# Two products of 256 columns in place of one of 512, three for the left half of the bank and then three for the right

## The reference, cut to what matters

```python
mix = jnp.einsum('btd,de->bte', merged, w_out[l])                   # first block: out projection
u = jnp.square(jax.nn.relu(jnp.einsum('btd,df->btf', n2, w_up[l])))
h = h + _rmsnorm(jnp.einsum('btf,fd->btd', u, w_down[l]), ...)      # F = 4096
...
mix = jnp.einsum('bse,ed->bsd', ..., w_o[layer])                    # second block, two layers
ffn = swiglu(x, w_gu_dense, w_down_dense)                           # layer 0, F = 2816
out = out + gates[..., e:e + 1] * swiglu(x, w_gu[e], w_down[e])     # layer 1, e = 0..7, two gates non-zero per token
```

## Time and profile before

| | |
|---|---|
| median of 3 runs | 1766.68 us |
| the profiled execution, its own time | 1765.85 us |
| its span in the profile | 1764.0 us |
| PE busy | 1740.7 us, 99% |
| PE weight loads busy | 1566.5 us, 89% |
| DVE busy | 1360.9 us, 77% |
| ACT busy | 1074.3 us, 61% |
| products of L449 to L451 with 512 columns | 3 x 1226 |
| of these in the experts (992 us to the end) | 3 x 992 |

### The profile page before, as it was taken

How to read it: one execution, slowest core, us unless ns; L and a number is a source line. 1 busy time by engine, 2 the same in 40 slices (tenths; PEclk the granted TensorE clock), 3 DMA queues, 4 the chain that set the end, 5 groups by cost and what they waited for, 6 DMA issues and landing times.

```text
span 1764.0 us, 26421 instructions
## 1 busy us (share of the span) xinstructions
PE 1740.7 (99%) x11201; PEld 1566.5 (89%) x11201; DVE 1360.9 (77%) x1586; ACT 1074.3 (61%) x1200; POOL 187.6 (11%) x191
## 2 busy tenths in 40 slices
PE   8999999999999999999999999999999999999997
PEld 8999999999988999998997888788888888888885
DVE  6895488677664667655687899888889898989897
ACT  7654455565544444443346778777777776777774
POOL 1454170000000100000030202100000000000110
PEclk9999999999999999999999999999999999999998
DMA  9332464656556545565463599999999999999993
GB/s 290 120 109 73 118 179 133 224 174 199 181 190 202 187 153 188 189 227 181 144 200 132 209 388 345 384 408 408 372 385 356 398 367 398 355 384 359 392 409 140
DMA packets 179542, 452.11 MB, mean 256 GB/s; under 512 B 11813, under 2 KB 119816, under 8 KB 145496
## 3 DMA queue, kind: packets, MB, share of 16 engines
q1 hardware_dynamic: 176424, 440.37, 69.3%
q0 software_dynamic: 2992, 9.98, 1.4%
HBM read 442.14 MB, written 5.79 MB: 254 GB/s over the span
## 4 chain that ended last, share of the span: by engine, by line
PE 89%; DVE 6%; ACT 3%; DMA 1%; issue 1%; SPq 0%; DVEq 0%; ACTq 0%
PE bank L449 27%; PE bank L451 27%; PE bank L450 27%; DVE ring_r L439 2%; PE bank L3283 1%; ACT hi_ring L424 1%; DMA ring<-in_expert_blocks 1%; PE bank L2545 1%; PE bank L1371 1%; PE bank L1363 1%; DVE arena L946 1%; PE bank L1855 1%; PE bank L2526 0%; PE bank L1840 0%; PE bank L2175 0%
## 5 line engine op out<-in xcount | busy, mean ns | idle before, releaser
L439 DVE TENSOR_TENSOR ring_r<-ring,hi_ring 128x2048 fp32r<-128x2048 f32 x401 | 905.7, 2283 | 257.2 <-ACT hi_ring L424 256.9
L424 ACT CAST hi_ring<-ring 128x2048 fp32r<-128x2048 f32 (+1 forms) x404 | 758.2, 1905 | 120.6 <-PE bank L451 108.8
L449 PE MATMUL bank<-hi_ring,arena_r 128*128 128x512 f32 (+1 forms) x1526 | 570.8, 374 | 1.9 <-DVE ring_r L439 1.8
L450 PE MATMUL bank<-ring_r,arena_r 128*128 128x512 f32 (+2 forms) x1534 | 566.2, 369 | 0.0
L451 PE MATMUL bank<-hi_ring,arena_r 128*128 128x512 f32 (+1 forms) x1526 | 564.9, 370 | 0.0
L449 PE MATMUL bank<-ring_r,hi_ring 128*128 128x256 f32 (+1 forms) x1400 | 398.3, 285 | 0.3 <-DVE ring_r L508 0.3
L451 PE MATMUL bank<-ring_r 128*128 128x256 f32 (+1 forms) x1400 | 394.1, 282 | 0.0
L450 PE MATMUL bank<-ring_r,hi_ring 128*128 128x256 f32 (+1 forms) x1400 | 393.1, 281 | 0.0
L449 PEld LDWEIGHTS bank<-hi_ring,arena_r 128*128 128x128 f32 x1526 | 286.5, 188 | 53.9 <-DVE ring_r L439 5.9
L451 PEld LDWEIGHTS bank<-hi_ring,arena_r 128*128 128x128 f32 x1526 | 286.6, 188 | 49.8
L450 PEld LDWEIGHTS bank<-ring_r,arena_r 128*128 128x128 f32 (+1 forms) x1534 | 287.8, 188 | 48.0
(11 more groups left out here) (444 smaller groups left out, 1584.1 us busy)
## 6 DMA issues: line engine op xcount, KB each, us to landing
ring<-in_expert_blocks SPq DMA_DIRECT2D x264, 1024.0 KB, 6.7
ring<-in_w_in SPq DMA_DIRECT2D x31, 1024.0 KB, 5.6
ring<-in_w_gu_dense SPq DMA_DIRECT2D x22, 1024.0 KB, 5.2
ring<-in_w_up SPq DMA_DIRECT2D x16, 1024.0 KB, 5.5
ring<-in_w_down SPq DMA_DIRECT2D x16, 1024.0 KB, 5.1
ring<-in_w_in_a SPq DMA_DIRECT2D x10, 1024.0 KB, 5.9
ring<-in_w_down_dense SPq DMA_DIRECT2D x10, 1024.0 KB, 5.0
ring<-in_w_o SPq DMA_DIRECT2D x8, 1024.0 KB, 5.1
```

Of the source, the lines that this page charges most:

```text
L424: q.e.copy(hi_ring[:, b:b + m], ring[:, a:a + m]).then_inc(*q.did(("hi", of.tag, i)))
L439: q.e.tensor_tensor(ring_r[:, a:a + m], ring[:, a:a + m], hi_ring[:, b:b + m].bitcast(F32), ALU.subtract).then_inc(*q.did(("lo", of.tag, i)))
L449: q.e.matmul(ps, a[0], b[0], start=first, stop=False)
L450: q.e.matmul(ps, a[0], b[1], start=False, stop=False)
```

## The change

A product of `mm3` whose target has 512 columns is given as two calls of `mm3` with 256 columns each: first the three products for the left half of the bank, then the three for the right half. The stationary operands are the same for both, and each of the six instructions has its weight load. Only the very first product of the left half opens the bank, only the last one of the right half closes it, and that last one is also the one that carries the semaphore.

```diff
     def mm3(q, ps, a, b, first, last):
+        if ps.shape[-1] == 512:
+            mm3(q, ps[:, 0:256], a, (b[0][:, 0:256], b[1][:, 0:256]), first, False)
+            return mm3(q, ps[:, 256:512], a, (b[0][:, 256:512], b[1][:, 256:512]), False, last)
         q.e.matmul(ps, a[0], b[0], start=first, stop=False)
         q.e.matmul(ps, a[0], b[1], start=False, stop=False)
         return q.e.matmul(ps, a[1], b[0], start=False, stop=last)
```

## The result

The changed kernel takes 1783.72 us (median of 4 runs, 1782.45 to 1784.17), the kernel before beside it 1767.93 us. The ratio is 1.0109, with a 95% interval of 1.0090 to 1.0128: slower by 16 us, 1.1%. The profiled execution has 1783.32 us and a span of 1781.4 us, 17.4 us over the span before.

The account below looks back on a forecast made before the run. PE was taken as the bound, busy for 1740.7 of 1764.0 us. The terms 24.1 - 3.3 - 1.5 = +19.3 us, taken as +20, gave 1787 us, with 1776 to 1795 for 8 in 10.

Parts of the forecast that it names:

- PE sets the end, and a product's price is the distance of starts: Whole kernel: PE is busy 1740.7 of 1764.0 us; products cost their start distance, 229.0 ns for 512 columns, 117.8 for 256.
- +6.6 ns per product, +24.1 us: All 3678 touched products: two of 256 columns cost 2 x 117.8 - 229.0 = +6.6 ns more, +24.1 us.
- A tenth at the faster level, -3.3 us: New 256-column products: a tenth run at the faster 113.3 ns, taking 3.3 us off.
- Waits given back, -1.5 us: Experts: PE's 1.8 us of waits for DVE's split weights should go; 1.5 us given back, between 0 and 3.
- Half banks 0: Changing the half bank after each three products costs 0; the far end would be 221 us.
- gaps behind transposes 0: Gaps of some 90 ns behind transposes stay as before, 0; else 4 us given back or as much cost.
- The rule of 2.5 ns per product: Page's N / 2.4 + 2.5 ns per product: the split would cost an estimate of 9.2 us; not used in the sum.
- The rule of its Part 3: Added weight loads, all using all rows, would be exposed: an estimate of 392 us; the prediction said the trace disagrees.
- The instruction queue: Rival: some 30 more packets, 60 in the experts each half a microsecond late, +30 us, 1817; 0.09 together with half banks.
- The faster level throughout: Rival: new products run at 113.3 ns nearly everywhere, experts too; -9.0 us, median 1758 us; chance 0.04.
- the mixed lock: Rival: half of the products at each of 117.8 and 113.3 ns; +6 us, 1773 us; chance 0.07.

Follow-up runs that it names:

- the second comparison: Changed kernel run once more, no edit, beside the kernel before: 1784.94 us against 1763.13 us, ratio 1.0124.
- unequal: Changed kernel split unequally: 320 + 192 columns in the rows, 384 + 128 in up products, 448 + 64 in down products; 1975.95 us.

## Why the prediction was right, and where only its sum was

The prediction said +20 us, 1787 us with 1776 to 1795. Measured were 1783.72 us and +15.8 us, with +21.8 in the second comparison; the two profiles are 17.4 us apart. Step by step:

- **PE sets the end, and a product's price is the distance of starts.** Shown: 117.8 ns in the experts after, with the rest of the engines unchanged, and the cost in proportion to the number split (15.4 and 4.6 us).
- **+6.6 ns per product, +24.1 us.** Right as a difference of two levels. That it is a price per product and not one of order or bank halves is shown by the two other orders. Its make-up was open: 5.0 of the 6.6 ns stay with loads of half the size. The other 1.6 ns go with the size of the load or with the partitions written.
- **A tenth at the faster level, -3.3 us.** The step that failed, though the sum doesn't show it. Of the 2452 new groups only 59 were fast, 2.4%: -0.8 us. In its place untouched groups changed their level: -3.4 us in the one stretch that takes either level by itself, as the second profile of the kernel before shows, and +1.1 in others. That makes -2.3, and -3.1 with the 0.8: near the -3.3 by luck.
- **Waits given back, -1.5 us.** The right size for waits, but something is left. Gaps of more than 0.12 us beyond the usual distance, between products of `mm3` in the experts, fall from 3.0 us (seven) to 1.3 us (four). With the shorter gap that follows most of them this is some 2 us of the 2.8; the rest, and the 0.8 before the experts, have no cause shown. The late block of the earlier trace rows did not come back in the experts after.
- **Half banks 0, gaps behind transposes 0.** Both are shown. Behind the transposes the first two products are 316 ns apart before and 202 ns after (medians over 39 places in the experts), 87 and 84 ns beyond the usual distance:

```profile
1210.35 0.60 PE L3286 MATMUL bank<-consts,arena 128*128 128x128 f32 x4
1210.70 0.36 PE L452 MATMUL bank<-hi_ring,arena_r 128*128 128x256 f32 x1
1210.90 0.28 PE L453 MATMUL bank<-ring_r,arena_r 128*128 128x256 f32 x1
1211.02 0.28 PE L454 MATMUL bank<-hi_ring,arena_r 128*128 128x256 f32 x1
```

- **The rule of 2.5 ns per product** (the Trainium skill, "TensorE: Matmul & The Clock Gate", section "Back-to-back issue gap", which gives it as the gap of an isolated product) would have given an estimate of 9.2 us. The runs have 4 to 5 ns per product with small loads and 6.6 with full ones, so the trace differs. The rule of its Part 3 that a load overlaps only with products of another row group does not hold here: 3678 more loads, on all rows, cost 16 us in all.
- **Rivals.** The instruction queue took 119 packets for 90, 29 more where some 30 were estimated, and PE is busy through all of the stretches above; the four long gaps of the experts, 1.3 us in sum, leave no room for 30 us. The faster level throughout did not happen: 59 of 1984 groups in the experts. Nor did the mixed lock.

## What to carry to other kernels

Where PE is the bound, price a split of products by the distance of starts in stretches of each width, not by busy time or columns alone: here each product more, with a load of its own, costs 6.6 ns (4 to 5 with loads of 64 columns), whatever the order. Do not go below the width that covers a weight load. With 128 stationary columns that is some 110 ns: products of 256 columns were above it (117.8 ns), those of 192 and fewer were held to it wherever one stood behind another, and the wide product behind them was late in starting its successor. And profile a kernel twice before putting 3 us down to a change.

## What the runs showed of the hardware that was not expected

- Products of 256 columns run at 117.8 or at 113.3 ns from start to start, at the full granted clock. The stretch of 255 groups kept one level throughout and had either in executions of the same program. What chooses the level stays open.
- Weight loads of 128 columns start 107 to 113 ns apart and no closer in a stream of short products (`unequal`). Behind three short products a long one starts its successor late, after 229 instead of 175 ns at 384 columns and after 288 instead of 201 at 448. With loads of 64 columns it doesn't (173 ns at 384).
- Besides columns at 2.4 GHz and a price per product there is a part that grows with the columns. With small loads the distances are 60.4, 116.7, 173 and 228.4 ns for 128, 256, 384 and 512 columns: 56 ns for each 128 more, where 2.4 GHz would give 53.3. What makes it isn't shown.
